# One-hot products of a PEER layer moved beside the first U blocks, built per token in fp32, with one token tile of a running sum kept at a time

## The reference, cut to what matters

```
q = (ht @ w_pq).reshape(t, 8, 2, 128)
s = einsum('thcd,hcnd->thcn', q, sub_keys)       # 128 keys on each of 2 sides
v1, i1 = top_k(s[:, :, 0], 16); v2, i2 = top_k(s[:, :, 1], 16)
cv, ci = top_k(v1[..., :, None] + v2[..., None, :], 16)
e = i1[ci // 16] * 128 + i2[ci % 16]; g = softmax(cv)
a = einsum('ckd,cd->ck', u_emb[e], h)            # 128 experts for each token
out = einsum('ck,ckd->cd', gelu(a) * g, v_emb[e]); x = x + out
```

## Time and profile before

| | |
|---|---|
| median of three runs | 4191.82 us |
| span of the profiled execution (the page gives no other time of it) | 4193.2 us |
| PE, DVE, ACT, POOL busy | 85%, 74%, 34%, 20% |
| picks stage of half 0 / of half 1 | 2416 to 2595 / 3212 to 3327 us |
| U stage of half 0 (32 blocks) / of half 1 (64 blocks) | 2595 to 2842 / 3327 to 3809 us |
| V stage of half 0 / of half 1 | 2842 to 3206 / 3809 to 4180 us |

### The profile page before, as it was taken

How to read it: one execution, slowest core, us unless ns; L and a number is a source line. 1 busy time by engine, 2 the same in 40 slices (tenths; PEclk the granted TensorE clock), 3 DMA queues, 4 the chain that set the end, 5 groups by cost and what they waited for, 6 DMA issues and landing times.

```text
span 4193.2 us, 60957 instructions
## 1 busy us (share of the span) xinstructions
PE 3546.2 (85%) x22046; PEld 3217.2 (77%) x22046; DVE 3103.5 (74%) x3905; ACT 1421.7 (34%) x1936; POOL 835.7 (20%) x772
## 2 busy tenths in 40 slices
PE   7997988852996338978888867999998999999998
PEld 6876987752775228976888857997887999998886
DVE  4654444468898777877789999887787777777786
ACT  4544433321443113333432201334442233333443
POOL 0000000000223543222111266222221012121221
PEclk9999998986998668989999956999998699999999
DMA  5651655532998888989877856998886188888887
GB/s 188 193 162 51 181 152 174 176 110 107 355 333 318 302 317 329 362 321 329 314 266 289 297 179 210 337 360 311 330 329 245 55 320 313 302 313 307 327 332 293
DMA packets 288251, 1099.78 MB, mean 262 GB/s; under 512 B 24832, under 2 KB 25216, under 8 KB 219008
## 3 DMA queue, kind: packets, MB, share of 16 engines
q1 hardware_dynamic: 208640, 528.55, 37.1%
q0 software_dynamic: 73728, 536.90, 33.8%
q10 hardware_dynamic: 5760, 32.80, 2.1%
HBM read 1087.67 MB, written 10.49 MB: 262 GB/s over the span
## 4 chain that ended last, share of the span: by engine, by line
PE 63%; DVE 14%; issue 11%; DMA 4%; POOL 4%; ACT 2%; DVEq 0%; ACTq 0%; PEldq 0%; POOLq 0%; PEld 0%; SPq 0%
PE ps L1083 17%; PE ps L1135 13%; PE ps L1307 13%; PE ps L1079 9%; PE ps L1280 5%; PE ps L1118 4%; POOL rows L305 3%; DVE rows L638 3%; DMA w<-v_emb 2%; DVE w_lo L655 2%; DVE pick L981 1%; DMA w<-w_out 1%; DVE w_lo L622 1%; ACT w_hi L327 1%; DMA gvec<-g_ffn_b 1%
## 5 line engine op out<-in xcount | busy, mean ns | idle before, releaser
L622 DVE TENSOR_TENSOR w_lo<-w,w_hi 128x1024 fp32r<-128x1024 f32 x752 | 918.9, 1224 | 642.4 <-ACT w_hi L327 589.9
L327 ACT ACTIVATE w_hi<-w 128x1024 fp32r<-128x1024 f32 x752 | 795.9, 1060 | 1244.6 <-PE ps L1083 375.3
L303 POOL TENSOR_TENSOR tick<-iota 128x1 f32<-128x1 f32 x256 | 167.8, 655 | 3201.0 <-DVE acc L642 1246.0
L638 DVE CUSTOM_DVE_ANT_0 rows<-rows,h 128x2048 f32<-128x2048 f32 x256 | 583.6, 2284 | 33.2 <-DMA rows<-u_emb,stage_i 31.2
L642 DVE SCALAR_TENSOR_TENSOR acc<-rows,stage_d,acc 128x2048 f32<-128x2048 f32 x256 | 600.3, 2345 | 6.5 <-DVE stage_d L633 5.4
L655 DVE TENSOR_TENSOR w_lo<-ps,w_hi 128x1024 fp32r<-128x1024 f32 x256 | 312.2, 1220 | 170.4 <-ACT w_hi L394 167.6
L394 ACT ACTIVATE w_hi<-ps 128x1024 fp32r<-128x1024 f32 x256 | 262.9, 1028 | 434.5 <-PE ps L1118 421.7
L305 POOL DMA_INDIRECT rows<-v_emb,stage_i x256 | 348.9, 1363 | 57.4 <-issue 39.3
L305 POOL DMA_INDIRECT rows<-u_emb,stage_i x256 | 318.8, 1246 | 57.7 <-issue 41.0
L1135 PE MATMUL ps<-ht_hi,w_lo 128*128 128x256 f32 x2048 | 292.3, 286 | 37.8 <-DVE w_lo L655 37.5
L1079 PE MATMUL ps<-w_lo,ht_hi 128*128 128x512 f32 x1024 | 281.3, 397 | 40.7 <-DVE w_lo L622 40.7
(11 more groups left out here) (180 smaller groups left out, 5157.5 us busy)
## 6 DMA issues: line engine op xcount, KB each, us to landing
w<-w_in SPq DMA_DIRECT2D x320, 512.0 KB
w<-u_emb SPq DMA_DIRECT2D x256, 512.0 KB
w<-v_emb SPq DMA_DIRECT2D x256, 512.0 KB
w<-w_out SPq DMA_DIRECT2D x64, 512.0 KB
w<-w_pq SPq DMA_DIRECT2D x64, 512.0 KB
w<-w_br_b SPq DMA_DIRECT2D x32, 512.0 KB
xin<-x ACTq DMA_DIRECT2D x4, 2048.0 KB, 8.9
w<-w_br_a SPq DMA_DIRECT2D x16, 512.0 KB
```

What stands on the lines that cost most here:

```text
L327: act.activation(w_hi[:, j % 2, :, :], w[:, j % RING, :, :], ACT.Copy).then_inc(hi_ready, 1)
L622: dve.tensor_tensor(w_lo[:, j % 2, :, :], w[:, j % RING, :, :], w_hi[:, j % 2, :, :].bitcast(F32), ALU.subtract).then_inc(lo_ready, 1)
L638: dve.tensor_tensor_reduce(out=row, in0=row, in1=h2[0][:, t, :], scale=1.0, scalar=0.0, op0=ALU.mult, op1=ALU.add, accum_out=stage_d[:, j: ...
```

## The change

The picks stages are gone. A *window* of the first eight U blocks (16 slabs) of each half now carries the products: behind each slab's U products PE does the products of 16 tokens, four at a time. `pick1` and `pick2` are plain fp32, so there is one product for a token and no split weight; DVE builds them token by token with two `tensor_scalar` instructions whose scalars are columns of `sel_t`. The gelu of the window's blocks goes to a buffer `held` and is multiplied into `coefs` behind the window. The window holds one turn for each slab; the counts of turns are 16, 48, 64 in half 0 (window, U, V) and 16, 64, 48 in half 1, where they were 32, 48, 48 and 0, 80, 48. `acc` holds one token tile: it is loaded at the start of each half and written at its end, where it was loaded and written once with both tiles.

```diff
-SPAN = 8
+SPAN = 4
-G_TURNS, U_TURNS, V_TURNS = TOK // SPAN, (48, 80), 48
+WIN = 8
+W_SLABS = 2 * WIN
+SUBS = TOK // SPAN
+PER = SUBS // W_SLABS
+W_TURNS, U_TURNS, V_TURNS = 16, (48, 64), (64, 48)
-    acc = at("acc", R_H2, [NT, D], F32)
+    acc = at("acc", R_H2, [D], F32)
+    held = at("held", R_H2 + 8192, [WIN, TOK], F32)
-    pick1 = at("pick1", R_SPLIT, [2, 2, SPAN, HB], F32R)
-    pick2 = at("pick2", R_SPLIT + 8192, [2, SPAN, NKEYS], F32R)
+    pick1 = at("pick1", R_RAW + 71680, [2, SPAN, HB], F32)
+    pick2 = at("pick2", R_RAW + 65536, [2, SPAN, NKEYS], F32)
...  ACT
+            def turned_hi(h, b0, G, j):
+                act.wait_ge(u_turned, G + (2 * (HB * h + b0) + 1))
+                act.wait_ge(slab_done, G + (table_g0[h][0] + 2 * b0 + 1))
+                act.activation(w_hi[:, j % 2, :, :], ps[:, 2 * (j % 2):2 * (j % 2) + 2, :], ACT.Copy).then_inc(hi_ready, 1)
+            def u_window(h, b0):
+                k0 = b0
+                for j in range(W_SLABS):
+                    turned_hi(h, b0, j, j)
+                    if j % 2 == 0 and j:
+                        activate(h, b0 + j // 2 - 1, (j // 2 - 1) % 2, held[:, j // 2 - 1, :])
+                    for q in range(PER):
+                        sub = PER * j + q
+                        act.wait_ge(picks_free, SUBS * h + sub + 3)
+                        act.activation(coefs[:, k0:, SPAN * sub:SPAN * (sub + 1)],
+                                       ps[:, 6 + sub % 2, 0:SPAN * HB].rearrange("p (m k) -> p k m", m=SPAN)[:, k0:, :], ACT.Copy).then_inc(spread, 1)
...  ACT, start of a half
                 if h == 0:
-                    act.dma_start(acc[:, :, :], yr[0]).then_inc(x1_back, 16)
                 else:
                     act.wait_ge(y_half, 16)
+                    act.wait_ge(acc_out, 16)
+                act.dma_start(acc[:, :], yr[0][:, h, :]).then_inc(x1_back, 16)
+                u_window(h, b0)
+                u_late(h, b0 + WIN, HB - b0 - WIN)
...  ACT, end of a half
                 act.dma_start(yr[1], total[:, :, :]).then_inc(y_half, 16)
+                act.wait_ge(acc_done, h + 1)
+                act.dma_start(yr[0][:, h, :], acc[:, :]).then_inc(acc_out, 16)
...  DVE
+                dve.wait_ge(x1_back, 16 * (h + 1))
+                def make_picks(sub):
+                    c = sub % 2
+                    dve.wait_ge(picks_free, SUBS * h + sub + 1)
+                    for m in range(SPAN):
+                        tok = SPAN * sub + m
+                        dve.tensor_scalar(pick2[:, c, m, :], iota[:, :], sel_t[:, 1, tok:tok + 1], None, ALU.is_equal)
+                        ins = dve.tensor_scalar(pick1[:, c, m, :], iota[:, HB * h:HB * h + HB], sel_t[:, 0, tok:tok + 1],
+                                                sel_t[:, 2, tok:tok + 1], ALU.is_equal, ALU.mult)
+                    ins.then_inc(picks_ready, 1)
+                for j in range(W_SLABS):
+                    split_turned(table_g0[h][0] + 2 * b0 + j, j)
+                    for q in range(PER):
+                        sub = PER * j + q
+                        make_picks(sub)
+                        if h == 0 and sub >= 2:
+                            weigh_early(sub - 2)
+                        if q == 1:
+                            turn(K0 + j // 8, j % 8, 1, h)
+                dve.wait_ge(spread, SUBS * (h + 1) + 2)
+                dve.wait_ge(a_free, HB * h + b1 + 1)
+                dve.tensor_tensor(coefs[:, b0:b1 - 1, :], coefs[:, b0:b1 - 1, :], held[:, 0:WIN - 1, :], ALU.mult)
...  PE
+                def spread_picks(sub):
+                    c = sub % 2
+                    pe.wait_ge(picks_ready, SUBS * h + sub + 1)
+                    pe.wait_ge(spread, SUBS * h + sub + 1)
+                    if h == 0:
+                        pe.wait_ge(weighed, sub + 1)
+                    for m in range(SPAN):
+                        ins = pe.matmul(ps[:, 6 + c, m * HB:(m + 1) * HB], pick2[:, c, m, :], pick1[:, c, m, :], start=True, stop=True)
+                    ins.then_inc(picks_free, 1)
                 turn_block(0, 0)
+                if window:
+                    for j in range(W_SLABS):
+                        turn_block(j + 1, j + 1)
+                        project(j, j // 2, j)
+                        for q in range(PER):
+                            spread_picks(PER * j + q)
```

More of the change, by code:

```diff
@@ L399, in u_blocks, with u_late, late, blocks @@
                     blocks(i)
-                activate(count - 1, 1)
+                activate(0, b0 + count - 1, 1, out(b0 + count - 1))
+            def u_window(h, b0):
[9 more added lines that the diff above has]
+                                       ps[:, 6 + sub % 2, 0:SPAN * HB].rearrange("p (m k) -> p k m", m=SPAN)[:, k0:, :], ACT.Copy).then_inc(spread, 1)
+            def u_late(h, b0, count):
+                def late(b, par):
+                    act.wait_ge(c_made, b + ((HB - EARLY - WIN) * h - b0 + 1))
+                    activate(h, b, par, ge[:, par, :])
+                def blocks(i, first=False):
+                    for j in range(2 * BODY):
+                        turned_hi(h, b0, i * (2 * BODY) + j, j)
+                        if j == 0 and first:
+                            activate(h, b0 - 1, 1, held[:, WIN - 1, :])
+                        elif j % 2 == 0:
+                            late(i * BODY + (b0 + j // 2 - 1), (j // 2 - 1) % 2)
+                blocks(0, True)
+                with act.Fori(1, count // BODY) as i:
+                    blocks(i)
+                late(b0 + count - 1, 1)
             n = 0
@@ L641, in turn @@
                     dve.wait_ge(used, n_ + ROWS)
-                    dve.scalar_tensor_tensor(acc[:, t, :], row, stage_d[:, j:j + 1], acc[:, t, :],
+                    dve.scalar_tensor_tensor(acc[:, :], row, stage_d[:, j:j + 1], acc[:, :],
                                              ALU.mult, ALU.add).then_inc(used, 1)
@@ L1005, in table @@
+                if h == 0:
+                    weigh_early(SUBS - 2)
+                    weigh_early(SUBS - 1)
                 def table(K0, rounds, count, n_turns, slab):
@@ L1120, in turn_block, with project @@
                     ins.then_inc(u_turned, 1)
+                def project(G, B, j):
+                    c, b = j % 2, j // 2
+                    if c == 0:
+                        pe.wait_ge(a_free, B + (HB * h + b0 + 1))
+                    for part, (wt, other) in enumerate(((w_hi, ht_hi), (w_hi, ht_lo), (w_lo, ht_hi))):
+                        if part == 0:
+                            pe.wait_ge(hi_ready, G + (g0 + 1))
+                        if part == 2:
+                            pe.wait_ge(lo_ready, G + (g0 + 1))
+                        for k in range(8):
+                            ins = pe.matmul(ps[:, 4 + b % 2, 0:TOK], wt[:, j % 2, k // 4, k % 4 * P:(k % 4 + 1) * P],
+                                            other[:, 8 * c + k, :], start=(c == 0 and part == 0 and k == 0),
+                                            stop=(c == 1 and part == 2 and k == 7))
+                    ins.then_inc(slab_done, 1)
@@ L1122, in blocks @@
                 def blocks(i, last=False):
                     for j in range(2 * BODY):
+                        G = i * (2 * BODY) + (W_SLABS + j if window else j)
                         if not (last and j == 2 * BODY - 1):
[L1125 to L1137 removed]
@@ L1271, in _ @@
                 enter(pe, "pe", n)
[L1272 to L1285 removed]
                 b0 = 0 if h else EARLY
[L1287 removed]
+                u_blocks(h, b0, HB - b0, True)
                 leave(pe, "pe"); n += 1
```

137 lines of the change are left out of this document (36 added, 101 removed).

## The result

| | before | changed |
|---|---|---|
| median of the runs | 4189.8 us | 4257.5 us |
| ratio to before | | 1.0156, 95% interval 1.0142 to 1.0171 |
| span of the profiled execution | 4193.2 us | 4250.7 us |
| forecast | | 4238 (4185 to 4315) |

The changed kernel is slower by 1.6%. The time came out 19.5 us above the forecast, inside its range and inside the range of its likeliest case.

A forecast was written before the change was run, and what follows sets the result against it. PE was taken to bound U and V, DVE half 0's picks, PE at half clock half 1's. Half 0 to V -13, V +11, half 1 +50, last write -3: +45 on 4193.2, about 4238 us (4185 to 4315).

The forecast's parts named there:

- likeliest case: Whole kernel: the prediction's own forecast, about 4238 us with its own range of 4205 to 4275; chance 0.58.
- the new wait: End of each window slab: DVE's w_lo waits for w_hi behind the last picks; DVE idle 2.5 to 3 us.
- the token: Window slabs: DVE's two narrow instructions for one token take 0.39 us, sixteen tokens 6.24 us.
- The upper bound: Window slabs: a token costs 0.50 us if narrow instructions are no shorter than 256 elements or the second scalar column costs more.
- the chain: Window slab's end: PE's last products, ACT's copy, w_hi and hand-overs; 3.0 us in half 0 with the weighing, 2.9 in half 1.
- U of half 0: Half 0 behind the window: held product 2 us, 48 slabs at 3.95 us making 190, last weigh and turn 4.
- V of half 0: V stage of half 0: 64 turns for 128 slabs ask 369 GB/s, 0.09 us a slab, +11 us (0 to 27).
- Half 1: Start of half 1: DVE waits for acc to be written and loaded again, idle some 15 us; half 1 in all +50.
- Break-even: Windows: token 0.36 us, short records and full clock give 4195 us, or 4174 if DMA hides its 21; chance 0.15.
- Faster: Windows: narrow instructions overlap their fixed part, only 0.07 us fixed, token 0.24; -77, 4161 us; chance 0.08.
- Slower still: Windows: token 0.50 us and half clock, 75 us more, with U and V another 33; 4313 to 4346 us; chance 0.13.
- POOL and DVE: Windows: gathers and DVE hold each other up; +30 us (4268) at 0.93 each, +6 at 0.19 each; chance 0.06.

The follow-up runs named there:

- e1: Against the changed kernel, the turn in each window slab stands behind the fourth span's picks instead of the second's; 4183.6 us, ratio 0.999 to the kernel before.
- g3: Against the changed kernel, the instruction building pick1 only compares, with one scalar column and no weighting; output not the reference's; 4233.4 us, ratio 1.0086 to the kernel before.
- g2: Against the changed kernel, PE does 20 products of zeros during each window turn; output not the reference's; 4244.9 us, ratio 1.0102 to the kernel before.
- g1: Changed kernel with e1's edit, wide one-hots and f4's edits, plus 48 turns beside V in half 0 instead of 64; 4126.2 us, ratio 0.9824 to before.
- e4: Against the changed kernel, acc is kept for both token tiles at once and loaded once; 4256.2 us, ratio 1.0156 to the kernel before.
- f4: Against e4, ACT in half 1 makes the first w_hi ahead of its wait for total's write; 4249.3 us, ratio 1.0140 to the kernel before.

## Why the prediction was right, and where it was off

**Right: the new wait.** The sum named DVE's wait for `w_hi` behind the last picks, 2.5 to 3 us a slab, as what makes the change lose. It is 3.35, ended by `w_hi`, and e1 shows that it is on the path: 2.33 us of work moved into it shortened the slab by 14.32 - 12.03 = 2.29. Three of the signs that the prediction named came a little outside their ranges: this wait (2.5 to 3), the slab of half 0 (14.3 against 13 to 14) and PE's share in the windows (74 and 79% against 55 to 70).

**Mis-sized: the token.** 0.39 us was taken, 0.42 measured (2441.32 - 2440.91 in the timeline above). The 128-element instruction came at 0.28 against 0.30; the 64-element one at 0.31 against 0.27, since its price was that of one with a single column; g3 puts 0.06 on the second column and its multiplication, not told apart. The upper bound, 0.50, had named the second column. Sixteen tokens: +0.5 us a slab.

**Mis-sized: the chain, and near by luck.** The 3.0 us at full clock hold the last `weigh_early` and DVE's idle time behind it; 0.4 was added for part of the time at half clock, 3.4 together in half 0. Measured are 0.20 + 3.35 = 3.55. g2, whose last records run at full clock, has 0.20 + 2.49 = 2.69, so the chain at full clock was put 0.3 too high: the eight records take 1.08 instead of 1.2, and ACT's copy overlaps `w_hi`, which starts 0.18 us after it and not 0.33. The clock costs 0.86 (3.35 - 2.49), twice the 0.4, because the chain runs at half clock in every slab of this window (all 15 waits are 3.35) and not for part of the time; the mean of 0.74 hides this. The two errors nearly cancel.

With these the slab of half 0 is 1.14 + 16 x 0.42 + 4 x 0.20 + 2.33 + 3.35 = 14.3 us, as measured; 13.7 was predicted. In half 1 it is 13.6 (the wait there is 3.39) against 13.1, where the prediction's own terms give 12.6 + 0.4 = 13.0. Sixteen of each make +18 us.

**The sum.** Between the two profiled spans lie +57.5 us, where +45 was predicted: 12.5 more. The windows make +18 of it; the other terms, right within a few us each, give some 5.5 back, so part of the small error is luck. The other 7 of the 19.5 us aren't in the mechanism: the changed kernel's profiled span, of the fastest of its four executions, lies 6.8 us under their median, where before's lay 1.4 above. The forecast says that it takes these 1.4 us off, but doesn't: 4193.2 + 45 - 1.4 is 4236.8.

**Right within a few us.** U of half 0: 192.8 us from the product by `held` to the last one, 196 predicted (2 + 190 + 4), with DMA full (share 0.97). V of half 0: +12.6 us, +11 predicted; g1 shows that the 16 more turns are the cause. Half 1: `w_lo` 22.2 us after the sum began, 21 predicted. The last write -1.6 instead of -3.

**Only half right: why half 1 starts late.** The text blamed `acc`. e4 takes it away and wins 5.1 of the 16 us; most of the rest is the wait for `total`'s write (f4 wins 8.2 more by moving it), which in the kernel before stood beside DVE's first two spans and in the changed one stands ahead of the first `w_hi`. The size was right because the term went through both.

**The rivals.** *Break-even* needed a token of 0.36 and full clock; neither came. *Faster* needed narrow instructions with a fixed part of 0.07 us from start to start. In g3, with one column each, the one of 128 elements takes 0.20 (2432.05 to 2432.25) and that of 64 takes 0.16 (2432.25 to 2432.41), so by a straight line some 0.12 are fixed; of their durations, 287 and 247 ns, 207 are. The Trainium skill (VectorE: DVE Perf Modes, "The TRN2 errata — SBUF-src ops pay a fixed extra latency per instruction") says that the extra of reading from SBUF is a fixed cost per instruction. A large fixed part agrees with it; that it comes from SBUF no run here shows. *Slower still* needed half clock throughout; the windows got 0.74 and 0.73. Of *POOL and DVE* something shows, but little. In half 0's window one narrow instruction beside each of the 16 gathers is longer by 0.06 to 0.11 us, as here:

```profile
2434.29 0.94 POOL L310 DMA_INDIRECT rows<-v_emb,stage_i  x1 [0.30 <-issue]
...
2434.89 0.38 DVE L1003 TENSOR_SCALAR pick<-iota,sel_t 128x128 f32<-128x128 f32 x1
```

The longest of both windows has 0.50 against 0.31. All this comes to some 3 us, half of the rival's smaller price of 6. The Trainium skill's rule of one port pair that fully blocks (SBUF — State Buffer, "SBUF: two separate sides") would hold DVE for POOL's whole 0.94 us if it bore on these instructions; the rows show nothing of that size.
